# Memory of the later stages placed once, next stage's first inputs loaded early, end waits moved to their readers

## The reference

```python
h = rms_norm(x, g) @ w_in                      # 1024 -> 5448 columns
p_r, p_a, g_r, g_a = split_cols(h)
y_r = rwkv7_branch(p_r, ...)                   # token shift, factors, recurrence over the rows, group norm
q, k, v, qi, wi, ki = dsa_project(p_a, pos)
y_a = attend(...)                              # prompt: index scores, best 256 keys of each query, attention
                                               # sample: the same over 8192 cached rows, found through a page table
merged = sigmoid(g_r) * (y_r @ w_br_rwkv) + sigmoid(g_a) * (y_a @ w_br_attn)
x = x + merged @ w_out
x = x + (gelu(conv3(a) + conv_b) * b) @ w_down # a, b = halves of rms_norm(x) @ w_up
```

## Time and profile before

| | us |
|---|---|
| median of 3 executions | 2869.07 (2864.42 to 2870.17) |
| the profiled execution, its own time | 2892.09 |
| its span in the trace | 2890.3 |
| busy in the span: PE | 2660.1 (92%) |
| DVE | 1542.0 (53%) |
| ACT | 807.0 (28%) |
| POOL | 273.3 (9%) |
| granted PE clock, mean over the span | 0.948 of 2.4 GHz |

### The profile page before, as it was taken

One profiled execution on the slowest core, in us unless ns is written; L12 is line 12 of the kernel. 1 busy time (PEld: TensorE's weight loads), 2 busy tenths in 40 slices (PEclk: granted clock), 3 DMA queues, 4 the chain that ended last, 5 costly groups with the idle time before them and its releaser, 6 DMA issues.

```text
span 2890.3 us, 45104 instructions
## 1 busy us (share of the span) xinstructions
PE 2660.1 (92%) x17968; PEld 1644.4 (57%) x17968; DVE 1542.0 (53%) x2834; ACT 807.0 (28%) x1791; POOL 273.3 (9%) x313
## 2 busy tenths in 40 slices
PE   8998999989985976889879999999979999999997
PEld 5554566656643322878745666655646665656664
DVE  2116888874333437667659999877823322221111
ACT  2215222015434453111112332013325321144411
POOL 0000111000000000000000222001344430000000
PEclk9998999999996986999989999999989999999999
DMA  5101112221104340000053232343355552523322
GB/s 208 32 13 37 61 69 83 69 61 43 39 24 168 120 125 25 4 26 11 11 196 111 102 116 105 121 140 134 118 176 170 188 186 84 182 95 114 119 96 74
DMA packets 86786, 278.53 MB, mean 96 GB/s; under 512 B 18488, under 2 KB 42648, under 8 KB 74224
## 3 DMA queue, kind: packets, MB, share of 16 engines
q1 hardware_dynamic: 74800, 224.58, 22.8%
q0 software_dynamic: 11776, 51.07, 5.5%
HBM read 242.72 MB, written 32.16 MB: 95 GB/s over the span
## 4 chain that ended last, share of the span: by engine, by line
PE 44%; DVE 1%; another core or an unknown queue 1%; issue 1%; DMA 1%; DVEq 1%; ACT 1%; POOL 0%; SPq 0%; ACTq 0%; POOLq 0%
PE tl_P L2002 22%; PE tl_P L2018 11%; PE tl_P L1964 4%; PE tl_P L1976 3%; PE tl_P L2048 1%; PE tl_P L2069 1%; PE tl_P L2037 1%; DVE tl_v L2308 0%; DVEq L2312 0%; PE tl_P L2029 0%; DMA tl_Z<-in_wb 0%; DVE tl_Z L2314 0%; PE tl_P L2031 0%; DMA out_y<-tl_YROW 0%
## 5 line engine op out<-in xcount | busy, mean ns | idle before, releaser
L2002 PE MATMUL tl_P<-tl_XN,tl_WU 128*128 128x368 f32 x2112 | 666.1, 477 | 14.9 <-issue 9.0
L2002 PEld LDWEIGHTS tl_P<-tl_XN,tl_WU 128*128 128x128 f32 x2112 | 403.8, 192 | 269.4 <-issue 24.8
L393 PE MATMUL dp_PS<-xT,dp_W 128*128 128x368 f32 x1440 | 455.7, 474 | 0.0
L393 PEld LDWEIGHTS dp_PS<-xT,dp_W 128*128 128x128 f32 x1440 | 270.7, 191 | 162.8 <-issue 3.7
L2018 PE MATMUL tl_P<-tl_HT,tl_WD 128*128 128x368 f32 x1056 | 332.1, 473 | 0.0
L2018 PEld LDWEIGHTS tl_P<-tl_HT,tl_WD 128*128 128x128 f32 x1056 | 199.0, 190 | 125.2 <-issue 4.1
L672 DVE TENSOR_SCALAR_CACHE_REDUCE dp_EQ<-dp_SCORE,dp_trial 16x1040 f32<-16x1040 f32 (+6 forms) x217 | 215.7, 994 | 21.8 <-issue 1.3
L148 PE MATMUL pa_PG<-pa_W,xT 128*128 128x402 f32 (+1 forms) x576 | 198.3, 504 | 8.2 <-DMA pa_W<-in_w_dsa 7.8
L148 PEld LDWEIGHTS pa_PG<-pa_W,xT 128*128 128x128 f32 (+1 forms) x576 | 106.6, 187 | 94.8 <-issue 14.3
L2308 DVE MAX8 tl_v<-tl_Z 128x8 f32<-128x4100 f32 x32 | 141.8, 4432 | 3.7 <-issue 1.9
L1964 PE MATMUL tl_P<-tl_Z 128*128 128x368 f32 x384 | 124.1, 485 | 20.7 <-DMA tl_Z<-in_wb 14.3
(11 more groups left out here) (380 smaller groups left out, 3464.0 us busy)
## 6 DMA issues: line engine op xcount, KB each, us to landing
tl_WU<-in_wu SPq DMA_DIRECT2D x66, 1024.0 KB
tl_WD<-in_wd SPq DMA_DIRECT2D x48, 704.0 KB
dp_W<-in_w_rw SPq DMA_DIRECT2D x15, 1024.0 KB, 5.0
tl_Z<-in_wb SPq DMA_DIRECT2D x24, 512.0 KB, 3.6
tl_Z<-in_wo SPq DMA_DIRECT2D x24, 512.0 KB, 3.6
gates<-dp_PX SPq DMA_DIRECT2D x16, 552.0 KB, 3.5
tl_Z<-gates SPq DMA_DIRECT2D x48, 184.0 KB, 3.6
PM_dram<-dp_PMT SPq DMA_DIRECT2D x14, 552.0 KB, 2.7
```

The source lines that it names most:

```text
L393: last = pe.matmul(bank(f)[:, 0:w], W[:, t // 2 % 2, k, 128 * (t % 2):128 * (t % 2) + 128], xT[:, k, c:c + w], start=k == 0, stop=k == KD - 1)
L2002: last = pe.matmul(out[:, 0:W], WU[:, i % 2, o:o + 128], XN[:, k, :], start=k == 0, stop=k == KD - 1)
```

## The change

All memory from stage 3 on is placed once: `base` (15876 columns) and `arena` (17664), of which `early`, `PML`, `F`, `PM` and the tail's tiles are views. What lies where another stage's data was is written once that data is dead, and each stage issues the next one's first loads. The waits at the stage ends go to those who first write over the sent memory.

- Stage 2: POOL gathers 0 and 1 run there (`QIT`'s and `xT`'s place); the shift rows are sent with the last `PM_dram` tile; the last attention store is no longer waited for, but by DVE in stage 3.
- Stage 3: no wait for the 20 stores at its end; ACT waits for them in stage 4, before it first writes `F["B"]`.
- Stage 4 also loads the six constant tiles of stage 5, behind its own loads.
- Stage 5: before piece b = 3 of its results SP loads `YT`, both `WM`, four `G`, two `XR` and `SC`; it ends without a wait for its stores. In stage 6 SP, POOL and (at unit 1) DVE wait for the last five of them.

```diff
+def gather_keys(pool, I, E, KX, kx_in, b):
+    pool.indirect_dma_start(
+        out=KX[b % 2], out_offset=None, in_=I["cache_kidx"],
+        in_offset=bass.IndirectOffsetOnAxis(ap=E["idx"][:, b:b + 1], axis=0)
+    ).then_inc(kx_in[b % 2], 16)
...
                         sp.dma_start(PM_dram[t], PMT[:, t % 2]).then_inc(pm_out[t % 2], 16)
+                        if t == NT - 1:
+                            sp.dma_start(shift_out, SH[:, :, :]).then_inc(sent, 16)
...
-                    sp.wait_ge(ya_out[i], 16 * ((NQ + 1 - i) // 2))
+                    sp.wait_ge(ya_out[i], 16 * ((NQ - 1) // 2))
                 sp.wait_ge(spilled[1], 32)
-                sp.dma_start(shift_out, SH[:, :, :]).then_inc(sent, 16)
...
                     pool.dma_start(P[16 * h:16 * h + 16, 3, :], SCORE[0:16, 0:TP]).then_inc(spread, 16)
+                pool.wait_ge(indexed, 1)
+                gather_keys(pool, I, E, KX, kx_in, 0)
+                pool.wait_ge(product, NU)
+                gather_keys(pool, I, E, KX, kx_in, 1)
...
                 sp.wait_ge(own_sent, 64)
-                for i in range(2):
-                    sp.wait_ge(sent[i], 2 * 80)
...
-                for b in range(NSEQ):
-                    if b >= 2:
-                        pool.wait_ge(woven, b - 1)
+                for b in range(2, NSEQ):
+                    pool.wait_ge(woven, b - 1)
+                    gather_keys(pool, I, E, KX, kx_in, b)
...
                 dve.tensor_copy(SCQ[:, :], PW[:, 0, 0:QS]).then_inc(own_placed, 1)
+                dve.wait_ge(ya_out[0], 16 * 5)
...
                 sp.dma_start(PM[:, 8:12], rows[:, 8:12]).then_inc(v_in, 16)
+                for n, src in (("masks", "masks"), ("seqm", "seqm"), ("lng", "lng"), ("pairs", "ones_pair"),
+                               ("hsum", "hsum"), ("hback", "hback")):
+                    sp.dma_start(pats[n][...], I[src]).then_inc(pats_in, 16)
...
                     act.wait_ge(a_done, u + 1)
+                    if u == 0:
+                        for i in range(2):
+                            act.wait_ge(sc_sent[i], 2 * 80)
...
                 for b in range(LASTB):
                     c, w = YC[b]
+                    if b == 3:
+                        sp.wait_ge(gram, 4 * SHORT)
+                        sp.wait_ge(padded, 1)
+                        sp.wait_ge(yr_out, 32)
+                        sp.dma_start(M["YT"][:, 0], yr_dram[:, :, 0:W3]).then_inc(soon["yr_in"], 16)
+                        for i in range(2):
+                            sp.dma_start(M["WM"][:, i, :], I["wb"][:, i]).then_inc(soon["wm_in"][i], 16)
+                            for j in range(2):
+                                sp.dma_start(M["G"][:, 2 * i + j, :], gates[KD * j + i][:, 0:W3]
+                                             ).then_inc(soon["g_in"][2 * i + j], 16)
+                            if i == 0:
+                                sp.dma_start(M["YT"][:, 1], ya_dram[:, :, 0:W3]).then_inc(soon["ya_in"], 16)
+                        for i in range(2):
+                            sp.dma_start(M["XR"][:, i, :], I["xt"][:, i, 0:W3]).then_inc(soon["xr_in"][i], 16)
+                        sp.wait_ge(y_done, SHORT)
+                        sp.dma_start(M["SC"], SC_dram).then_inc(soon["sc_in"], 16)
...
-                sp.wait_ge(sent, 16 * 7)
...
-                    sp.dma_start(YT[:, 0], yr_dram[:, :, col(g)]).then_inc(yr_in, 16)
-                    load_wm(16 * g)
-                    load_gate(16 * g)
-                    w = W if g < 2 else PW
-                    sp.dma_start(YT[:, 1, :, 0:w], ya_dram[:, :, W * g:W * g + w]).then_inc(ya_in, 16)
...
+                    else:
+                        sp.wait_ge(sent, 16 * 5)
+                        sp.dma_start(late[:, :], I["late"]).then_inc(late_in, 16)
+                        for dst, src in ((ones[:, :], I["ones_all"]), (gains, I["gains"])):
+                            sp.dma_start(dst, src).then_inc(small_in, 16)
...
             @block.gpsimd
             def _(pool):
+                pool.wait_ge(sent, 16 * 5)
                 pool.memset(AL[:, :], 0.0)
...
-                            dve.wait_ge(sc_in, 32)
+                            dve.wait_ge(sc_in, 16)
+                            dve.wait_ge(late_in, 16)
+                            dve.wait_ge(sent, 16 * 5)
...
+        KX = [early[:, 8832:12928], early[:, 0:4096]]
+        SCT = early[:, 4096:8192].rearrange("p (a r n) -> p a r n", a=2, r=4)
```

More of the change, by code:

```diff
@@ L797, with sample_scores @@
 HALF = (PAST + QS) // 2
-def sample_scores(nc, I, E, low, PM_dram, SC, ident):
+def sample_scores(nc, I, E, low, KX, SCT, kx_in, ya_out, sent, PM_dram, SC, ident):
     NR = 4 * 4
@@ L987, in _, with rwkv_factors @@
                 place(NR - 1)
-def rwkv_factors(nc, I, PM_dram, PM, low, F, PL):
+def rwkv_factors(nc, I, PM_dram, PM, low, F, PL, pats, pats_in, sc_sent):
     PML, wa2, vec = low["PML"], low["wa2"], low["vec"]
@@ L1192, in rwkv_chunks @@
         XP = sb("XP", [128, 5, 4, CH])
-        masks = sb("masks", [128, 18, CH])
+        masks, seqm, lng, pairs, hsum, hback = (
+            pats[n] for n in ("masks", "seqm", "lng", "pairs", "hsum", "hback"))
         RM, RN = (sb(n, [128, 3, 4, 128]) for n in ("RM", "RN"))
@@ L1766, in tail @@
         T = sb("T", [128, 2, 3, W + 2])
[L1767 to L1769 removed]
+        TOTAL = sb("TOTAL", [128, W])
         RS = sb("RS", [128, W])
@@ L2576, in program @@
-        tail(nc, I, S, SC, gates, yr_dram, ya_dram, O["v"], O["conv"], O["y"], ident)
+        base = sb("base", [128, 15876])
+        early, at_E, PML, vec = base[:, 0:13248], base[:, 13248:13640], base[:, 13640:15848], base[:, 15848:15876]
+        E = {"QB": at_E[:, 0:256].rearrange("p (a n) -> p a n", a=4), "KQ": at_E[:, 256:320],
+             "wcol": at_E[:, 320:324], "sel": at_E[:, 324:388].rearrange("p (a n) -> p a n", a=2),
+             "half": at_E[:, 388:389], "pt": sb("pt", [128, 8], I32), "idx": sb("idx", [128, 8], I32)}
@@ new lines, in program @@
+        low = {"PML": PML.rearrange("p (a n) -> p a n", a=2), "wa2": early[:, 8192:8704],
+               "vec": vec.rearrange("p (a n) -> p a n", a=7)}
+        xT = early[:, 0:KD * R].rearrange("p (k r) -> p k r", k=KD)
+        KX = [early[:, 8832:12928], early[:, 0:4096]]
+        SCT = early[:, 4096:8192].rearrange("p (a r n) -> p a r n", a=2, r=4)
+        F = {n: early[:, 4 * R * i:4 * R * i + 4 * R].rearrange("p (c r) -> p c r", c=4)
+             for i, n in enumerate(("B", "G", "RKK"))}
@@ new lines, in program, with sh @@
+        signals = lambda n, k: [nc.alloc_semaphore(name=f"{n}{i}") for i in range(k)]
+        kx_in, ya_out, sc_sent = signals("kx_in", 2), signals("ya_out", 2), signals("sc_sent", 2)
+        soon = {"wm_in": signals("wm_in", 2), "g_in": signals("g_in", 4), "xr_in": signals("xr_in", 2)}
+        soon.update({n: nc.alloc_semaphore(name=n) for n in ("yr_in", "ya_in", "sc_in", "sent")})
+        with ExitStack() as hold:
+            def sh(name, shape):
+                return hold.enter_context(nc.sbuf_tensor(name, shape, F32))
+            T = {"QT": sh("QT", [128, 4, R]), "QIT": early[:, 8832:13248].rearrange("p (c r) -> p c r", c=4),
+                 "KT": PML.rearrange("p (a n) -> p a n", a=2),
+                 "KIT": sh("KIT", [128, R]), "V": sh("V", [128, NB, 256]), "WI": sh("WI", [128, NB, 8])}
+            project_attention(nc, I, xT, ident, T, O["k"], O["v"], O["ki"], S)
+            prompt_and_project(nc, I, S, E, T, xT, KX, kx_in, ya_out, ya_dram, PM_dram, O["shift"], gates, ident)
@@ new lines, in program, with sr @@
+        sample_scores(nc, I, E, low, KX, SCT, kx_in, ya_out, sc_sent, PM_dram, SC, ident)
+        arena = sb("arena", [128, 16 * R])
+        PM = arena[:, :].rearrange("p (t r) -> p t r", t=16)
+        F["A"] = PM[:, 12:16]
+        M = merge_tiles(base, arena)
+        with ExitStack() as hold:
+            def sr(name, shape):
+                return hold.enter_context(nc.sbuf_tensor(name, shape, F32))
+            PL = sr("PL", [128, 4, 25])
+            pats = {"masks": sr("masks", [128, 18, CH]), "seqm": sr("seqm", [128, NSEQ]), "lng": sr("lng", [128, 4]),
+                    "pairs": sr("pairs", [128, 128]), "hsum": sr("hsum", [128, 4, 8]), "hback": sr("hback", [8, 4, 128])}
+            pats_in = nc.alloc_semaphore(name="pats_in")
+            rwkv_factors(nc, I, PM_dram, PM, low, F, PL, pats, pats_in, sc_sent)
+            rwkv_chunks(nc, I, PM, F, PL, pats, pats_in, M, soon, O["state_p"], O["state_s"], yr_dram, ya_dram, SC, gates,
+                        ident)
@@ L2579, in shape_constants @@
+        tail(nc, I, S, M, soon, gates, yr_dram, ya_dram, O["v"], O["conv"], O["y"], ident)
 def shape_constants():
```

178 lines of the change are left out of this document (76 added, 102 removed).

## The result

| | before | after |
|---|---|---|
| median of 5 timed runs each, us | 2869.07 (2864.42 to 2876.32) | 2845.74 (2843.72 to 2846.73) |
| ratio, 95% interval | | 0.9916 [0.9904, 0.9928] |
| profiled execution / its span, us | 2892.09 / 2890.3 | 2843.72 / 2841.9 |
| mean granted clock | 0.948 | 0.958 |

The change gained 23.3 us; 31.7 were forecast, and the range held it. The profiled executions lie 48.4 us apart. Half of that is not the change's: by the first `up` of group 2 (1982.76 before, 1958.60 after) they are 24.2 apart, and the rest comes behind it, where the profile of before has the hole of PE beside the cache gathers and this profile of after has none.

The account below looks back on a forecast made before the run. Transfers at four stage borders, a store landing before a load, were taken as what the change could shorten: 13.3 + 3.2 + 4.5 + 10.7 = 31.7 us off the 2869.07 median gives 2837.4 us, range 2829 to 2849.

Parts of the forecast that it names:

- The bound and the mechanism: Four stage borders: engines idle while a store must land and a load can only start afterwards; 31.7 us to gain.
- The price of a bare border: Stage change without an end wait: 0.83 us, read at border 4 to 5 and taken wherever the end wait goes.
- Border 2 to 3: No end wait and gathers 0 and 1 issued in stage 2: 13.3 us gained, 4.0 of them from the stage's earlier start.
- The ends 12.6 and 13.7: Range of the gain at border 2 to 3, in us, depending on how late gather 3 lands.
- Borders 3 to 4 and 4 to 5: 3.2 us from no wait for the score stores, 4.5 us from constant tiles loaded in stage 4.
- Border 5 to 6: Tail starts with data for four units in place and no wait for the last store: 10.7 us gained.
- Is it fed?: Tail start: the third weight tile lands 3.6 us after it is asked for, units 3 and 4 need 5.0: yes.
- Rival B: Tail gives back its gain, PE waiting for the third weight tile or a gate: 10.7 becomes about 5, 2843 us; 10%.
- SP's extra issues: Stage 5: twelve extra load issues, about 0.5 us each, between result pieces 2 and 4; nobody waits for SP, no cost.
- The cache-gather stretch: Tail: PE's 20 us idle beside POOL's cache gathers is untouched by the change, so the gain comes off the median.
- Rival D: Cache gathers in the tail: shifted DVE and PE lists starve PE longer, twice the extra (40 us), 2877 us; 2%.

Follow-up runs that it names:

- Run 7: Changed kernel with the three waits for the last stores put back at the ends of stages 2, 3 and 5; ratio to before 0.9945.
- run 8: Changed kernel with gathers 0 and 1 back in stage 3 and the six constant tiles loaded at stage 5's start; ratio to before 0.9960.
- run 2: Changed kernel with the tail's loads issued at the start of the tail instead of in stage 5; 2872.02 us, ratio to before 0.9907.
- run 1: The changed kernel measured again, no edit; 2865.95 us, ratio to before 0.9895.
- run 9: Kernel before plus only two waits that hold back POOL's third and fourth group of cache gathers; 2870.24 us, ratio to before 0.9999.
- run 4: Changed kernel plus a second burst of the tail's loads earlier in stage 5, from memory to memory, result unused; ratio to before 0.9937.
- run 5: Changed kernel plus two waits that hold back POOL's third and fourth group of cache gathers; 2849.77 us, ratio to before 0.9849.
- run 12: Repeat of run 5 (changed kernel, paced cache gathers, loads in one burst) on another chip; 2844.86 us, ratio to before 0.9897.
- run 11: Repeat of run 6 (changed kernel, paced cache gathers, spread loads) on another chip; 2839.77 us, ratio to before 0.9887.
- run 6: Changed kernel with paced cache gathers and the tail's loads spread over chunks 15 to 17 of stage 5; 2842.97 us, ratio to before 0.9835.

## Why the prediction was right, and where it was off

**The bound and the mechanism** were right: the path ran through the landing of a store and a load behind it at three borders, and through a load alone at 4 to 5. Run 7 measures the landings, run 8 the first inputs, run 2 the tail's preload (7.5), each near its expectation at the borders; the ratios of runs 7 and 8 lie 8 and 5 us beyond what the borders give.

**The price of a bare border**, 0.83 us, was small. From the end of the last store's issue to the row of the next stage shown above it took 1.40 (899.30 - 897.90), 0.96 (1031.43 - 1030.47) and 1.49 (1441.88 - 1440.39); only 4 to 5 repeated it (1124.10 - 1123.29 = 0.81). It had been read from one border, which had no store of SP's just ahead. In the sum that is 1.4 us too much.

**Border 2 to 3.** The ends 12.6 and 13.7 rested on gather 3 taking 9.2 us or a little more. It took 10.6, PE lacked 1.93 us instead of 0.56, and at the second pass 12.0 was kept. Later passes made it up: 13.3 at the stage's end here, while the other changed kernels with both gathers ahead need 132.6 to 135.8 us from the last attention store to the last score store, before 146.0: 10.2 to 13.4. By the fit of the Trainium skill (page "DMA: Bandwidth & Descriptors", section "Anatomy of one DMA — SWDGE (gpsimd) path"), 2.0 us plus the bytes at 436 GB/s, an estimate for such a gather is 6.8 us; 10.6 us doesn't agree with it.

**Borders 3 to 4 and 4 to 5** came out as worked out, 3.1 and 4.5.

**Border 5 to 6** gave 9.7 for 10.7. "Is it fed?" ("yes, by 1.4 us") held: 128 matmuls without a break. Rival B did not happen.

**The step that failed** is the last sentence of that part: SP's extra issues "stand between result pieces 2 and 4 ... nobody waits for SP there", so they were taken at nothing. Nobody does wait for SP. But they are 5.6 MB of transfers, and I asked only what they keep from SP's queue, not what they keep from PE: its instructions come late beside them, and its clock falls. That cost 4.8 us over seven profiles, 5.0 in this one, the largest single part of the 8.4 that the forecast was too high here. It doesn't explain the miss from run to run: run 1 pays the same 5 us and still gains 30.4.

**Open.** Of the other 3.8 us of stage 5 about half is more idles of the same kind (5.9 us in all put down to `issue` up to chunk 14, 4.0 before); the rest, and the 1.8 of stage 4, are not explained. Stages do wobble: the first matmul of stage 5 to chunk 14's U copy took 246.1 us before and 244.3 in run 9, 244.8 to 251.5 in the changed kernels (256.8 with run 4's second burst), and the longest (250.2 to 251.5; runs 1, 5, 7, 12) have a clock of 0.92 to 0.93, the shortest (244.3 and 244.8; 9, 11) one of 0.95 and 0.96. The last attention store of stage 2 goes at 901.7 in before and at 897.0 in run 9, whose stage 2 is the same code, so the 4.3 us gained there need no effect of the change. The change was worth 23.3 us in the first measurement, 30.4 in run 1 and 29.6 as run 12 has it; the forecast's 31.7 is near the latter two.

**The cache-gather stretch** was rightly left out of the sum: the gain came off the median, and the 23.0 us by which the profiled execution of before lay above it are near the 24.2 by which the two profiles part there. Rival D's lengthening was not seen: the stops sum to 14.7 us in before, and to 13.5 to 15.1 in the six changed profiles that have them.

## What to carry to other kernels

A load moved ahead "into idle time" has two prices: the queue that issues it, and the DMA engines that it fills. Here the preload saves 7.5 us at its border and costs 4.8 before it in one burst, 2.2 in pieces. Where PE runs many short instructions, spread such loads over the stretch in pieces, each behind some later step, and look for idles put down to `issue` and a lower clock beside a full DMA share. Then ask the DMA queues whether an instruction transfer ends just before each idle does: in stage 5 it always did, at the cache gathers never, and one name hid two causes. The best version here does both, spread loads and paced gathers: 0.9835 on the chip with the hole and 0.9887 on the one without, against 0.9895 for the change alone on a chip with it. And price a border from one that looks like it, with a store issued just ahead: here 1.0 to 1.5 us.

## What was not expected of the hardware

PE can stop without a wait for anything that the profile shows, and in two ways.

In stage 5 it stops until a transfer of its own instructions has landed. Every one of 74 stops above 0.6 us ended 1.2 to 1.6 us behind such a transfer. A burst of 5.6 MB makes these stops more and longer (1.3 and 2.0 us in after, up to 5.5 in run 4), with the instruction transfers starting 6.0 to 9.3 us apart instead of 3.5 to 4.8; writes to the on-chip memory are not needed for it (run 4). "Mostly hidden", as the Trainium skill's page "Runtime: NRT & Kernel Launch" (section "Instruction fetch mechanics") has it, holds in the quiet stretches, with 3 or 4 stops above 0.6 us beside 67 transfers, and not beside the burst.

Beside the cache gathers it stops for 14.3 us in ten stops in run 1, with no instruction transfer near and with the DMA engines less busy (0.70) than in the same work without a stop (0.85 in after). Runs 5 and 6 show that holding the third and fourth group of gathers back removes these stops on a chip whose unpaced kernels have them. What PE lacks there is not known.
